# Six homes for split expert-weight chunks, and down weights read as two neighbouring rows per partition

## The reference

```python
def expert_block(args):
    xblk, e = args
    hh = xblk @ w1[e] + b1[e]                       # w1[e]: 1024 x 2048
    glu = jnp.minimum(hh[:, :D_FF], SWIGLU_LIMIT)
    lin = jnp.clip(hh[:, D_FF:], -SWIGLU_LIMIT, SWIGLU_LIMIT)
    act = glu * jax.nn.sigmoid(SWIGLU_ALPHA * glu) * (lin + 1.0)
    return act @ w2[e] + b2[e]                      # w2[e]: 1024 x 1024
```

## Time and profile before

| | before |
|---|---|
| median of 3 runs | 2221.84 us (2213.68 to 2222.48) |
| profiled execution, its own time | 2221.01 us |
| span in the profile | 2219.2 us |
| mean granted TensorE clock | 0.986 |
| DVE busy over the span | 1734.6 us (78%) |
| of the span, experts' steady part | about 1200 to 2150 us |

### The profile page before, as it was taken

How to read it: one execution, slowest core, us unless ns; L and a number is a source line. 1 busy time by engine, 2 the same in 40 slices (tenths; PEclk the granted TensorE clock), 3 DMA queues, 4 the chain that set the end, 5 groups by cost and what they waited for, 6 DMA issues and landing times.

```text
span 2219.2 us, 29496 instructions
## 1 busy us (share of the span) xinstructions
PE 2132.5 (96%) x10033; PEld 1683.0 (76%) x10033; DVE 1734.6 (78%) x1668; ACT 1273.8 (57%) x1265; POOL 788.0 (36%) x293
## 2 busy tenths in 40 slices
PE   7999999999999999999999999999999999999996
PEld 3888888888887888788777777777777777777764
DVE  6756655655636866856879999999999999999996
ACT  6413222132223723732467888788888787888784
POOL 3000000000202023000614655657655557656575
PEclk9999999999999999999999999999999999999998
DMA  9322223132231021045689999999999999999994
GB/s 308 124 95 95 95 77 140 55 129 76 77 132 39 1 95 57 1 151 213 222 320 385 398 396 401 389 400 396 401 399 396 391 390 396 392 391 387 375 398 169
DMA packets 132755, 541.06 MB, mean 244 GB/s; under 512 B 13779, under 2 KB 22115, under 8 KB 98622
## 3 DMA queue, kind: packets, MB, share of 16 engines
q1 hardware_dynamic: 123336, 516.43, 60.6%
q0 software_dynamic: 9040, 19.30, 3.5%
q10 hardware_dynamic: 296, 4.21, 0.5%
HBM read 528.97 MB, written 19.82 MB: 247 GB/s over the span
## 4 chain that ended last, share of the span: by engine, by line
PE 74%; DVE 9%; DMA 7%; issue 6%; ACT 3%; POOL 1%; DVEq 0%; ACTq 0%; SPq 0%; POOLq 0%
PE ps L2423 70%; DMA raw<-in_exp_w 3%; DVE wlo L2168 3%; DVE hlo L2168 2%; DMA ar<-in_exp_w 2%; ACT hhi L1362 2%; PE ps L2770 1%; DMA ar<-h_d,ar 1%; DVE ylo L2320 1%; PE ps L2990 1%; DVE ar L2343 1%; POOL list_d L883 1%; PE ps L3005 1%; DMA ar<-in_ctx 0%; ACT hlo L1413 0%
## 5 line engine op out<-in xcount | busy, mean ns | idle before, releaser
L962 POOL DMA_INDIRECT out_x<-ar,cur x32 | 388.2, 12132 | 250.5 <-DVE ar L2343 189.8
L2423 PE MATMUL ps<-whi,yhi 128*128 128x512 f32 x800 | 293.9, 410 | 30.6 <-DVE wlo L2168 30.3
L2168 DVE TENSOR_TENSOR hlo<-raw,hhi 128x2048 fp32r<-128x2048 f32 x132 | 298.5, 2281 | 23.8 <-ACT hhi L1362 23.8
L2168 DVE TENSOR_TENSOR wlo<-raw,whi 128x2048 fp32r<-128x2048 f32 x132 | 296.9, 2277 | 0.2 <-ACT whi L1362 0.2
L1362 ACT ACTIVATE hhi<-raw 128x2048 fp32r<-128x2048 f32 x132 | 252.8, 1917 | 52.8 <-PE ps L2423 38.4
L828 POOL TENSOR_SCALAR sm<-ss 128x8 f32<-128x8 f32 (+3 forms) x39 | 13.2, 338 | 754.9 <-ACT ar L1185 487.6
L2423 PE MATMUL ps<-hhi,yhi 128*128 128x512 f32 x800 | 278.7, 394 | 0.1
L1362 ACT ACTIVATE whi<-raw 128x2048 fp32r<-128x2048 f32 x132 | 249.1, 1918 | 37.7 <-PE ps L2423 36.8
L1529 DVE TENSOR_TENSOR wlo<-raw,whi 128x2048 fp32r<-128x2048 f32 x56 | 128.2, 2289 | 159.4 <-ACT whi L1024 159.4
L2423 PE MATMUL ps<-whi,hhi 128*128 128x512 f32 x592 | 233.3, 394 | 0.0
L2423 PE MATMUL ps<-whi,hlo 128*128 128x512 f32 x592 | 230.8, 390 | 0.0
(11 more groups left out here) (378 smaller groups left out, 4517.5 us busy)
## 6 DMA issues: line engine op xcount, KB each, us to landing
raw<-in_exp_w SPq DMA_DIRECT2D x264, 1024.0 KB, 8.3
ar<-in_exp_w SPq DMA_DIRECT2D x132, 1024.0 KB, 9.0
raw<-in_w_in SPq DMA_DIRECT2D x44, 1024.0 KB, 5.0
raw<-in_w_mod SPq DMA_DIRECT2D x22, 1024.0 KB, 6.8
raw<-in_w_br_ret SPq DMA_DIRECT2D x8, 1024.0 KB, 5.2
ar<-in_x SPq DMA_DIRECT2D x8, 512.0 KB, 7.8
raw<-in_w_br_diff SPq DMA_DIRECT2D x4, 1024.0 KB, 5.0
raw<-in_w_out SPq DMA_DIRECT2D x4, 1024.0 KB, 9.6
```

What stands on the lines that cost most here:

```text
L962: pool.indirect_dma_start(a["out"], bass.IndirectOffsetOnAxis(ap=rows, axis=0), F(A_Y, D)[0:m], None, bounds_check=L - 1, oob_is_err=False ...
L2168: V.tensor_tensor(e_wlo[j % ESPL], e_raw[s], e_whi[j % ESPL].bitcast(F32), ALU.subtract).then_inc(e_lo, 1)
L2423: return pe.matmul(out, lhsT, rhs, start=start, stop=stop, skip_group_check=skip)
```

## The change

- Split chunks have six homes and not four (`ESPL = 6`). The two new pairs (`e_more`) lie in the arena, over data that item 0 is done with: the new rows (`A_XN`), the bias source (`A_BSRC`) and the routing tables (`A_RT`). Hence new waits in item 0: ACT's `hi_e(0, 4)` waits for `n2_done` and `stored`, `hi_e(0, 5)` for `bias_lo`, DVE's `lo_e(0, 5)` for all of `listed`; and ACT's `glu(0)` waits for `gathered` and `cur_ready`, since `A_GS` is moved. The list for wide items goes to an unused stretch of `cst`.
- The home of a chunk goes by its raw slot and no longer by `j % ESPL`.
- A `w2` chunk is loaded with two neighbouring rows to a partition, 8 KB in one piece, and not row p and row p + 128, 4 KB each. Partition p then holds rows 2p and 2p + 1 of the chunk's 256, so `turn_act` transposes every second column of the activations.
- In each item ACT and DVE do more chunks before `act_high`/`act_low` (five and not four), DVE's `give` comes after chunk 6 and not after chunk 3, chunk 11 comes before `activate` and `lower_up`, and `fold_y` on PE comes after the third up chunk.

```diff
-ESPL = 4
+ESPL = 6
 AHEAD = 2
+TURNED_AT, GIVE_AT = 5, 7
...
-A_XG, A_Y, A_GS, A_TH, A_AC = 0, 1024, 2048, 3072, 9216
+A_XG, A_Y, A_GS, A_TH, A_AC = 0, 1024, 14848, 3072, 9216
+A_SPLIT = (A_XN, A_BSRC), (A_XN + 2048, A_RT)
...
-                sp.dma_start(e_raw[raw_slot(i, j)].rearrange("p (a n) -> p a n", a=2),
-                             a["exp_w2"][one(e), k * 2 * P:(k + 1) * 2 * P, :].rearrange(
-                                 "o (a p) n -> p (o a) n", p=P)).then_inc(e_loaded[raw_slot(i, j)], 16)
+                sp.dma_start(e_raw[raw_slot(i, j)], a["exp_w2"][one(e), k * 2 * P:(k + 1) * 2 * P, :].rearrange(
+                    "o (p a) n -> p (o a n)", a=2)).then_inc(e_loaded[raw_slot(i, j)], 16)
...
                     act.wait_ge(tile_done, DONE_OUT + 2 * LT)
+                    if j == KH:
+                        act.wait_ge(n2_done, LT)
+                        act.wait_ge(stored, 16 * LT)
+                    if j == KH + 1:
+                        act.wait_ge(bias_lo, 2)
...
-                act.activation(e_whi[j % ESPL], e_raw[s], ACT.Copy).then_inc(e_hi, 1)
+                act.activation(e_whi[s], e_raw[s], ACT.Copy).then_inc(e_hi, 1)
...
+            act.wait_ge(gathered, 32)
+            act.wait_ge(cur_ready, 1)
             glu(0)
...
-                V.tensor_tensor(e_wlo[j % ESPL], e_raw[s], e_whi[j % ESPL].bitcast(F32),
+                if isinstance(i, int) and i == 0 and j == KH + 1:
+                    dve.wait_ge(listed, 16 * LT * TOP_K)
+                V.tensor_tensor(e_wlo[s], e_raw[s], e_whi[s].bitcast(F32),
...
-                                            F(A_AC, 2, COL)[0:m, hf, c * P:(c + 1) * P], ident[0:m, 0:m])
+                                            F(A_AC, 2, 2, P, 2)[0:m, hf, c // 2, :, c % 2], ident[0:m, 0:m])
```

More of the change, by code:

```diff
@@ L290, in build @@
         k_ctx = nc.alloc_sbuf_tensor_at("k_ctx", [P, 2, C], F32R, offset=ar_at + 4 * (A_TMP + 2 * L))
+        e_more = [[nc.alloc_sbuf_tensor_at(f"e_more{w}{k}", [P, KH, COL], F32R, offset=ar_at + 4 * A_SPLIT[w][k])
+                   for k in range(2)] for w in range(2)]
         ct = sb("ct", [P, 2, KC])
@@ L318, in F @@
                 return v
-            names = "abc"[:len(shape)]
+            names = "abcd"[:len(shape)]
             return v.rearrange("p (%s) -> p %s" % (" ".join(names), " ".join(names)),
@@ L1421, in item @@
             def item(i, half_b, half_a, half, half_n, n=None):
-                for j in range(AHEAD, ESPL):
+                for j in range(AHEAD, TURNED_AT):
                     hi_e(i, j)
-                if not (isinstance(i, int) and i == 1):
-                    write_sel2(i - 1)
                 if half_b:
@@ L1429, in item @@
                 act_high(i - 1, half_a)
-                for j in range(ESPL, MOE_N - 1):
+                if not (isinstance(i, int) and i == 1):
+                    write_sel2(i - 1)
+                for j in range(TURNED_AT, MOE_N):
                     hi_e(i, j)
-                write_sel(i + 1)
                 if half:
                     lower_up(i)
-                    hi_e(i, MOE_N - 1)
                     x_high(i + 1, half_n)
+                    hi_e(i + 1, 0)
                     glu_half(n)
@@ L1439, in item @@
                     glu(i)
-                    hi_e(i, MOE_N - 1)
+                    hi_e(i + 1, 0)
                     x_high(i + 1, half_n)
-                for j in range(AHEAD):
-                    hi_e(i + 1, j)
+                write_sel(i + 1)
+                hi_e(i + 1, 1)
             def item_at(i):
@@ L1479, in _ @@
             act.activation(bias2, b2, ACT.Copy).then_inc(b2_hi, 1)
-            for j in range(ESPL, FIRST):
+            for j in range(KH, FIRST):
                 hi_e(0, j)
@@ L2346, in item @@
             def item(i, half_b, half_a, half, half_n, buf_b, n=None, n_b=None):
-                for j in range(AHEAD, ESPL):
+                for j in range(AHEAD, TURNED_AT):
                     lo_e(i, j)
                 act_low(i - 1, half_a)
+                for j in range(TURNED_AT, GIVE_AT):
+                    lo_e(i, j)
                 if half_b:
@@ L2354, in item @@
                     give_y(i - 2, chunk(i - 1, MOE_N - 1), buf_b)
-                for j in range(ESPL, MOE_N - 1):
+                for j in range(GIVE_AT, MOE_N):
                     lo_e(i, j)
                 if half:
-                    lo_e(i, MOE_N - 1)
                     x_low(i + 1, half_n)
-                    activate_half(i, n, lambda: lo_e(i + 1, 0))
-                    lo_e(i + 1, 1)
[L2362 to L2366, removed]
+                    lo_e(i + 1, 0)
+                    activate_half(i, n, lambda: lo_e(i + 1, 1))
+                else:
+                    activate(i, lambda: lo_e(i + 1, 0))
+                    x_low(i + 1, half_n)
+                    lo_e(i + 1, 1)
             def item_at(i):
@@ L2407, in last_low @@
                 give_half(end - 1, end, None)
-                for j in range(AHEAD, ESPL):
+                for j in range(AHEAD, MOE_N - FIRST):
                     lo_e(end + 1, j)
@@ L3100, in fold_before @@
                 def fold_before(kk):
-                    if half_b and kk == 1:
+                    if half_b and kk == 2:
                         fold_y(n_b)
@@ L3154, in last_down @@
                     for q in range(2):
-                        last = down_chunk(k, 2 * k + q, ps[:, 2 + c, :], c, True)
+                        last = down_chunk(raw_slot(end + 1, k), 2 * k + q, ps[:, 2 + c, :], c, True)
                     if k == MOE_N - FIRST - 1:
```

16 lines of the change are left out of this document (8 added, 8 removed).

## The result

| | before | after |
|---|---|---|
| median (4 runs each, same chip) | 2218.2 us | 2247.92 us (2245.82 to 2250.2) |
| ratio to before | 1 | **1.0132** [1.0111, 1.0153] |
| span in the profile | 2219.2 us | 2248.2 us |
| mean granted clock | 0.986 | 0.979 |

A forecast was written before the change was run, and what follows sets the result against it. The prediction took the 16 DMA engines as the bound, with DVE 4% behind. 24.4 us for the w2 pieces plus 2 us for item 0 made 26.4 us off 2221.0: 2195 us, range 2182 to 2213.

The forecast's parts named there:

- The bound: Steady part, 1200 to 2150 us: the 16 DMA engines bound the kernel at 33.2 us an item, DVE 4% behind.
- w2 in 8 KB pieces: w2 loads run at w1's 421 GB/s, not 384: 0.96 us an item, 0.74 coming through, 24.4 us over 33 items.
- The second rival: w2 loads: the piece size isn't why they are slow; only start and homes gain, about 2217 us; chance 0.15.
- the sum's main term: Loads of w2 in 8 KB pieces: 24.4 of the 26.4 us forecast as gain.
- Strided transposes: PE's transposes of every second column: taken as 0, at most 0.85 us an item if a step doubled them.
- The homes: Six homes by themselves: nothing to win in the steady part, at most 2 us from 1130 to 1200 us.
- The third rival: POOL's gather comes late because DVE runs without gaps: 2235 us, with no cover 2321; chance 0.07.
- The point from which it decides: POOL's gather: lateness decides once its issue ends later than about 25 us after the `turn_x` before it.
- The price of a wait: Late gather, each pair of items: 7.9 us lost, 5.4 carried by two new homes, 2.5 us remaining.
- Item 0: New waits at the start: 2 us of gain, between a loss of 2 us and a gain of 5.2 us.
- The order within an item: Moved steps in the loop: no instruction added, longest DVE run of chunks down from seven to five; counted as 0.

The follow-up runs named there:

- e5: Kernel before with only w2 loaded in 8 KB pieces, transposes unchanged (output not the layer's): 2222.06 us, ratio 1.0002.
- e6: Kernel before with only the transposes changed to every second column, w2 still in 4 KB pieces (output not the layer's): 2233.81 us, ratio 1.0040.
- e9: Kernel before with six homes alone, old order, 4 KB pieces and transposes of neighbouring columns: 2300.76 us, ratio 1.0326.
- e2: Changed kernel with w2 in 4 KB pieces and transposes of neighbouring columns again; six homes and new order stay: 2254.89 us, ratio 1.0151.
- e14: e9 with POOL's copy of the next rows moved ahead of the scatter: 2212.96 us, ratio 0.9961 to the kernel before.
- e13: e10 plus the strided PSUM reads of e12, without a stop of DVE: 2202.67 us, ratio 0.9919 to the kernel before.
- e3: Changed kernel with only four homes in use (ACT waits for the chunk four places earlier, not six): 2240.53 us, ratio 1.0093.
- e1: Kernel before with 8 KB w2 pieces and the strided transposes, four homes and old order: 2232.68 us, ratio 1.0051.
- e10: Changed kernel with POOL's copy of the next rows moved ahead of the scatter: 2211.0 us, ratio 0.9927 to the kernel before.
- e7: Changed kernel, DVE waiting for POOL's gather behind the second step of activate, once per narrow item: 2212.96 us, ratio 0.9947 to the kernel before.
- e12: e7 with ACT's sigmoid and DVE's first activate step reading every second PSUM column, so transposes read neighbouring ones: 2206.56 us, ratio 0.9905.
- e17: e13 with the second step of activate right behind the first in narrow items, next item's chunk 1 after both: 2198.51 us, ratio 0.9893.
- e4: Changed kernel, DVE waiting in each narrow item for POOL's gather ahead of the second step of activate: 2238.79 us, ratio 1.0081.
- e8: e7 with even and odd activation columns put apart by strided writes, so transposes read neighbouring columns: 2245.74 us, ratio 1.0097.

## Why the prediction was wrong

- **The bound, the step that failed first.** "The share never leaves 1 and a queue stands before it: the 16 DMA engines are the bound." e5 made the transfers faster and the time stayed (1.0002); e6 gave PE 7.6 us more in the stretch and the time grew by as much for 33 items (8.9 us). PE set the pace of the kernel before, at 914.2 of 950 us busy, and its 35.8 us of waits and the slow stretches of its clock were part of the item's 33.2 us. Whether DVE, busy 911.0 us, set it as well, no run shows by itself. The DMA share hid this: it is 1.01 at 395 GB/s and still 0.99 at 378, with 7.5 us from issue to landing for 2.89 us a chunk, so that more than two loads are still in flight at a time. PE busy 914 and the wait of 29.5 us for DVE stood in the earlier trace rows and were read as slack.
- **w2 in 8 KB pieces: 24.4 us, came to 0.** The piece was the cause of a third of the gap between 384 and 421 (395 in e5), and none of it reached the end. The second rival (2217) had the right time for this part for another reason. With the pace set by PE, the sum's main term had nothing to come from.
- **Strided transposes: 0, came to 8.9 us.** The bound from above was 0.85 us for an item, the measured one 0.27. It was set to nothing because "PE isn't the bound".
- **The homes: nothing or 2 us, came to a loss of 3.3%** alone (e9). The third rival named the mechanism, with 2235 us and 2321 without cover; the whole change gave 2248 and e9 2301. What was argued against it failed: "POOL now has four or five places in an item where DVE reads PSUM and not three". The gather stood through two of them, `act_low` and `give`, and went out in a gap. It wasn't DVE's idle time as a whole that counted: that rose, from 39 to 72 us in the stretch. In e9 it was one gap of 1 us, ahead of the last chunk before `x_low`, which the homes closed; in the new order the scatter and the copy get out behind it, at `x_low` and at the first step of `activate`, and the gather, starting 0.16 us ahead of the next chunk, doesn't. The point from which it decides was put some 4 us too early, at 25 us after `turn_x`: in the kernel before an issue that ended 29.6 us behind it cost PE 0.48 us, in the changed one 33.4 us cost 3.8.
- **The price of a wait.** The rival reckoned 2.5 us for a pair. PE's waits grew by 56.9 - 35.8 = 21 us in the stretch, and PE's busy time for a chunk from 2.665 to 2.715 us, 16 us over 329 chunks, of which the strides are some 7 us; the rest goes with the clock's 0.97 for 0.99. Together they are, within 2 us, the 14 missing chunks of 2.77 us.
- **Item 0: 2 us of gain, came to 6.6.** DVE stopped 1.02 us for `listed` or ACT, the gather of item 1 took 3.59 us of issue and not 12.40, PE didn't wait for it, and from 1100 to 1200 PE is busy 99.9 us where it was 93.3. The step was right, its size low; two homes more may help here too, but no run parts the two.
- **The order within an item: 0, which held with six homes only.** There the old order is the worse one (e9 and e2; e14 and e13, by 0.5%). With four in use the new order cost 0.4% (e3 and e1).

## What to carry to other kernels

A DMA share of 1 with a queue before it doesn't make the DMA engines the bound where the issuer always keeps loads ahead; change one resource at a time, as a faster transfer alone (e5) and more work for TensorE alone (e6) did here, and see which of them the time follows. When more buffers close an engine's gaps, ask who lived on them: GpSimd got its scatter out in a gap of VectorE, and with that gap closed its gather came late. A copy moved out of the way (e10) or one short stop of VectorE (e7) each turned the loss of 1.3% into a gain of about 0.5%; the 1.1% of the best kernel also needs the reads of e12 and the order of e17. A stop costs by its place: the same one two instructions earlier made 0.8% slower and not 0.5% faster.

## What the runs showed of the hardware

- A gather that takes POOL 1.06 us to issue takes 26.1 us while DVE is busy without a gap, and then ends 0.86 us after DVE falls idle. Which DVE instructions let POOL through isn't settled. The second step of `activate`, with both inputs in SBUF, did in some pairs of e7 (issue ended 0.94 us after its start) and in none of the 13 pairs of the changed kernel; `act_low` let a copy through in the kernel before and not in e4. In e10 the first step, out of PSUM, let five gathers out 0.94 us after its start and not nine others that had begun at the same point. The kind of instruction alone doesn't decide it.
- A transpose of 128 columns that reads every second fp32 column takes PE 284 ns and not 250, as a mean over both forms.
- Out of PSUM, ACT and DVE read every second fp32 column for nothing (1025 and 1222 ns for 1024 columns in e12, 1023 and 1224 with neighbouring columns in the changed kernel), but writing fp32 to places 512 B apart takes 2126 and 2107 ns (e8).
- After a wait of 3.8 us of PE the granted clock was 0.66 over the next 5 us; over the stretch the seven kernels with 0.95 to 0.97 had a wait of PE of 2.0 to 6.8 us on average once for each pair of items, the others, with 0.98 to 1.00, of at most 2.3 us. Waits of 2.0 to 2.3 us stand on both sides, and what parts these isn't shown.
